# Attention scores with 64 rows of depth: two units at a time in TensorE's row halves

## What is computed

```
# first block: 8 heads of 64, three dilation patterns, written in the kernel as one masked softmax
scores = jnp.einsum('bhrnqd,bhrnkd->bhrnqk', qb, kc)
# even layer: 4 heads, each with two components of 64, and one context of 768 keys
def diff_attend(q, k, v, lam, scale):
    s = jnp.einsum('bqhcd,bkhcd->bhcqk', q, k).astype(jnp.float32) * scale
    p = jax.nn.softmax(s, axis=-1)
    w = (p[:, :, 0] - lam * p[:, :, 1]).astype(v.dtype)
    return jnp.einsum('bhqk,bkhd->bqhd', w, v)
```

## Time and profile before

| | us |
|---|---|
| median of 3 runs | 2516.4 |
| lowest and highest of them | 2516.34, 2520.65 |
| span of the profiled execution | 2514.0 |
| AT1, about | 219 to 315 |
| ATA, about | 596 to 706 |

### The profile page before, as it was taken

How to read it: one execution, slowest core, us unless ns; L and a number is a source line. 1 busy time by engine, 2 the same in 40 slices (tenths; PEclk the granted TensorE clock), 3 DMA queues, 4 the chain that set the end, 5 groups by cost and what they waited for, 6 DMA issues and landing times.

```text
span 2514.0 us, 26493 instructions
## 1 busy us (share of the span) xinstructions
PE 2214.4 (88%) x10170; PEld 1251.6 (50%) x10170; DVE 1298.6 (52%) x2310; ACT 978.0 (39%) x1609; POOL 459.6 (18%) x512
## 2 busy tenths in 40 slices
PE   6998998999888986999999997779999788777777
PEld 2444544446566444766676664446665333222222
DVE  2147526437875147889888985366662411111111
ACT  2024323114554035887888783355552100000000
POOL 0000000000133111454545420032221000000000
PEclk9999999999999997999999999889999889999999
DMA  7122611101000358999999997400032699999998
GB/s 279 67 74 93 226 44 38 67 17 68 1 1 1 135 222 301 358 370 367 373 378 367 380 357 282 171 8 1 1 134 103 248 382 404 407 404 404 402 412 345
DMA packets 92570, 546.29 MB, mean 217 GB/s; under 512 B 7807, under 2 KB 10639, under 8 KB 67614
## 3 DMA queue, kind: packets, MB, share of 16 engines
q1 hardware_dynamic: 84894, 521.02, 53.1%
q0 software_dynamic: 6144, 20.98, 3.7%
q10 hardware_dynamic: 1408, 2.62, 0.3%
HBM read 523.62 MB, written 20.97 MB: 217 GB/s over the span
## 4 chain that ended last, share of the span: by engine, by line
PE 23%; DMA 15%; DVE 11%; ACT 6%; issue 4%; POOL 1%; another core or an unknown queue 0%; SPq 0%; ACTq 0%; POOLq 0%; DVEq 0%
DMA AR<-in_w_exp_up_dram 8%; DVE RW L2087 7%; PE PS L2342 5%; PE PS L2121 5%; DMA AR<-in_w_exp_down_dram 4%; PE PS L684 3%; ACT AR L2175 3%; ACT RW L2079 2%; PE PS L985 2%; DMA AR<-in_w_exp_gate_dram 2%; PE PS L898 2%; PE PS L695 2%; PE PS L2536 1%; DVE AR L2294 1%; PE PS L2688 1%
## 5 line engine op out<-in xcount | busy, mean ns | idle before, releaser
L2087 DVE TENSOR_TENSOR RW<-AR,RW 128x2048 fp32r<-128x2048 f32 x192 | 432.5, 2285 | 45.6 <-ACT RW L2079 45.6
L2342 PE MATMUL PS<-AR 128*64 128x512 f32 x1536 | 363.1, 619 | 94.6 <-DMA AR<-in_w_exp_gate_dram 45.7
L2079 ACT CAST RW<-AR 128x2048 fp32r<-128x2048 f32 x192 | 364.1, 1912 | 121.0 <-PE PS L2121 107.4
L2121 PE MATMUL PS<-RW,RX 128*96 128x512 f32 x1536 | 363.1, 395 | 4.5 <-DVE RX L2227 4.0
L2121 PEld LDWEIGHTS PS<-RW,RX 128*96 128x96 f32 x1536 | 247.9, 162 | 110.7 <-issue 5.2
L2342 PEld LDWEIGHTS PS<-AR 128*64 128x64 f32 x1536 | 112.3, 141 | 321.2 <-issue 253.3
L2121 PE MATMUL PS<-RW,RA 128*96 128x512 f32 x768 | 186.6, 399 | 11.9 <-DVE RA L2284 11.9
L1713 PE MATMUL PS<-AR 128*128 128x512 f32 (+1 forms) x480 | 190.0, 552 | 0.7 <-ACT AR L620 0.7
L684 PE MATMUL PS<-AR 96*128 96x512 f32 (+3 forms) x480 | 183.5, 499 | 3.8 <-POOL AR L661 2.3
L784 DVE TENSOR_REDUCE AR<-PS 128x1 f32<-128x768 f32 (+1 forms) x160 | 135.9, 850 | 97.0 <-PE PS L684 78.7
L2419 POOL DMA_INDIRECT x_rows<-AR x16 | 119.0, 7439 | 351.7 <-DVE AR L2294 264.3
(11 more groups left out here) (346 smaller groups left out, 2684.3 us busy)
## 6 DMA issues: line engine op xcount, KB each, us to landing
AR<-in_w_exp_gate_dram SPq DMA_DIRECT2D x64, 2048.0 KB, 13.9
AR<-in_w_exp_up_dram SPq DMA_DIRECT2D x64, 2048.0 KB, 13.2
AR<-in_w_exp_down_dram SPq DMA_DIRECT2D x63, 2048.0 KB, 13.0
AR<-in_w_ada_dram SPq DMA_DIRECT2D x30, 2048.0 KB, 11.8
AR<-in_w_in_dram SPq DMA_DIRECT2D x6, 2048.0 KB, 9.1
AR<-in_w_in_even_dram SPq DMA_DIRECT2D x4, 2048.0 KB, 7.8
AR<-in_w_out_dram SPq DMA_DIRECT2D x2, 2048.0 KB, 7.9
AR<-in_w_out_even_dram SPq DMA_DIRECT2D x2, 2048.0 KB, 7.9
```

What stands on the lines that cost most here:

```text
L2079: s.copy(pair(i)[0], raw_half(key, hf)).then_inc(*S.up("hi", l, i))
L2087: v.tensor_tensor(lo, raw_half(key, hf), hi.bitcast(F32), ALU.subtract).then_inc(*V.up("split", key, hf))
L2121: m = pe.matmul(bank(ob)[0:Mc, :], st_, mv[:, k, 512 * q_:512 * q_ + 512], start=(k0 + k == 0 and n_ == 0), stop=(k0 + k == 7 and n_ == 2))
L2342: m = pe.matmul(bank(b)[64 * q_:64 * q_ + 64, :], op, w[:, c, 512 * q_:512 * q_ + 512], start=(h == 0 and c == 0), stop=(h == 1 and c == 3 ...
```

## The change

`pool_attn` and the cells are gone, and the two components (or two heads) of one query block are issued together by a new function. In an even step it waits for the banks of both units, and then issues for each slice of 512 keys one matmul of the upper unit with 64 rows at `tile_position` (0, 0) and one of the lower unit at (64, 0), into banks 0 or 1 and 2 or 3. Nothing is done for the scores in an odd step. In AT1 the order of units changes so that the two heads of a pair alternate within each query block: 128, 128, 256, 256, 384, 384, 512, 512 keys in place of 128, 256, 384, 512. The work of DVE and ACT on a unit, and their own order of steps, stay.

```diff
-        def pool_attn(A):
-            for i, u in enumerate(A.units):
-                r_ = u["row"]
-                if u["cell_before"]:
-                    G.wait_ge("full", "sc", *u["cell_before"])
-                u["ready"](G)
-                G.wait_ge("qz", 0)
-                g.tensor_copy(u["cell"][64 * r_:64 * r_ + 64, :], u["q"]).then_inc(*G.up("qp", A.tag, i))
+        def pe_scores_two(A, i):
+            for n_ in (i, i + 1):
+                u, p0 = A.units[n_], 2 * (n_ % 2)
+                K.fill(p0, "sc", A.tag, n_)
+                if u["nk"] > 512:
+                    K.fill(p0 + 1, "sc2", A.tag, n_)
+                    K.n[p0 + 1] -= 1
+                u["ready"](P)
+            nk = A.units[i]["nk"]
+            for a in range(0, nk, 512):
+                e_ = min(nk, a + 512)
+                m = [pe.matmul(PS[:, 2 * r_ + a // 512, 0:e_ - a], A.units[i + r_]["q"], A.units[i + r_]["k"][:, a:e_],
+                               start=True, stop=True, tile_position=(64 * r_, 0)) for r_ in range(2)]
+            for r_ in range(2):
+                m[r_].then_inc(*K.full("sc", A.tag, i + r_))
...
         def pe_attn(A, fill=None):
             n = len(A.units)
             for step in range(n + 4):
-                if step < n:
-                    pe_scores(A, step)
+                if step < n and step % 2 == 0:
+                    pe_scores_two(A, step)
...
-        for h in range(8):
-            for j in range(4):
-                r0, c = 64 * (h % 2), h // 2
-                units.append(dict(q=qT[r0:r0 + 64, c, 128 * j:128 * j + 128], k=kT[:, c, :], row=h % 2, vo=r0,
+        for h, j in [(2 * hp + r_, j) for hp in range(4) for j in range(4) for r_ in range(2)]:
+            r0, c = 64 * (h % 2), h // 2
+            units.append(dict(q=qT[r0:r0 + 64, c, 128 * j:128 * j + 128], k=kT[r0:r0 + 64, c, :], vo=r0,
...
-                    units.append(dict(q=QK[64 * c:64 * c + 64, h, 128 * j:128 * j + 128], k=QK[:, 4 + h, k0:k0 + nk],
-                                      row=c, nk=nk, dv=128, ready=QK_ready, vready=VV_ready,
+                    units.append(dict(q=QK[64 * c:64 * c + 64, h, 128 * j:128 * j + 128], k=QK[64 * c:64 * c + 64, 4 + h, k0:k0 + nk],
+                                      nk=nk, dv=128, ready=QK_ready, vready=VV_ready,
...
             g.memset(RB0, 0.0).then_inc(*G.up("rb0", 0))
-            pool_attn(AT1)
-            pool_attn(ATA)
             pool_pairs(ATB, lambda it: None)
```

More of the change, by code:

```diff
@@ L670, in pe_scores @@
             u["ready"](P)
-            if u.get("row") is not None:
+            if u.get("khl"):
                 P.wait_ge("qp", A.tag, i)
-            q = u["cell"] if u.get("row") is not None else u["q"]
-            if u.get("khl"):
                 at = 0
@@ L683, in pe_scores @@
                     e_ = min(nk, a + 512)
-                    m = pe.matmul(PS[:, p0 + a // 512, 0:e_ - a], q, u["k"][:, a:e_], start=True, stop=True)
+                    m = pe.matmul(PS[:, p0 + a // 512, 0:e_ - a], u["q"], u["k"][:, a:e_], start=True, stop=True)
             m.then_inc(*K.full("sc", A.tag, i))
@@ L1459, in program @@
         units = []
-        for h in range(8):
-            for j in range(4):
-                r0, c = 64 * (h % 2), h // 2
-                units.append(dict(q=qT[r0:r0 + 64, c, 128 * j:128 * j + 128], k=kT[:, c, :], row=h % 2, vo=r0,
-                                  nk=128 * (j + 1), moff=384 - 128 * j, dv=64, ready=qk_ready, vready=vv_ready,
-                                  v=lambda k, h=h: vv[:, k, 128 * (h // 2):128 * (h // 2) + 128],
-                                  out=OO[:, j, 64 * h:64 * h + 64]))
+        for h, j in [(2 * hp + r_, j) for hp in range(4) for j in range(4) for r_ in range(2)]:
+            r0, c = 64 * (h % 2), h // 2
+            units.append(dict(q=qT[r0:r0 + 64, c, 128 * j:128 * j + 128], k=kT[r0:r0 + 64, c, :], vo=r0,
+                              nk=128 * (j + 1), moff=384 - 128 * j, dv=64, ready=qk_ready, vready=vv_ready,
+                              v=lambda k, h=h: vv[:, k, 128 * (h // 2):128 * (h // 2) + 128],
+                              out=OO[:, j, 64 * h:64 * h + 64]))
         def fine(l, j):
```

## The result

| | before | after |
|---|---|---|
| median, us | 2516.37 | 2548.58 |
| lowest and highest | 2514.02, 2520.65 | 2546.02, 2551.27 |
| span of the profiled execution | 2514.0 | 2549.3 |

The ratio is 1.0124 (95% interval 1.0108 to 1.0139): 32 us slower. I had forecast 2530 (2518 to 2543), so the direction was right, the size less than half of what came, and the time lies outside the range.

A forecast was written before the change was run, and what follows sets the result against it. PE was taken to bound AT1, PE and DVE nearly both ATA. 2514.0 (span) + 2.4 (to the median) - 4 (AT1) + 11.3 - 0.8 + 2.8 + 0.5 + 4 (ATA) = 2530.2 us; range 2518 to 2543.

The forecast's parts named there:

- What bounds the kernel: PE sets the pace in AT1; in ATA PE and DVE are both close to full, with DVE next.
- the loop in ATA: Pair's scores wait for the second exponential, DVE for the scores: wide head 5.74 us against 4.93, +11.3 us in all.
- Splits: Four ATA heads with a key split: DVE waits longer for ACT, 4 x 0.7 = +2.8 us.
- those terms: ATA without the clock: wide heads +11.3, first pair's earlier start -0.8, key splits +2.8, narrow heads +0.5 us.
- Side by side: A pair's two row halves run at once: 1.3 us for a wide pair, against 2.6 without overlap.
- Rival 1: Row halves take turns: ATA's wide part +13, narrow +3, AT1 about +3, fewer clock falls; 2551 us, chance 0.12.
- The clock: PE's gaps in ATA cause four more falls to 1.2 GHz at 1 us: +4 us, between 0 and 9.
- AT1: First attention: scores save 3.6 net, a load costs 0.7, the start gains 1.0: -4 us, between -8 and 0.
- the order of units: In AT1, a load issued when fill work frees its slot makes PE wait about 0.7 us more.
- the waits behind ACT: In AT1, second transposes wait for ACT's copy: some 0.15 us in three of four pairs, 0.4 in 8 units.
- Rival 2: ATA's new wait costs little, the clock stays up, AT1 gives its whole 8 us: about 2519 us, chance 0.14.
- Rival 3: In ATA the pair's scores lie under DVE's own work, head 4.6 us: -5, AT1 -4; 2507 us, chance 0.06.

The follow-up runs named there:

- e3: e2 plus unread 128-column matmuls in PE's gaps of ATA (3 and 5 per wide head, 2 and 4 per narrow one): 2531.5 us.
- e2: The kernel before with paired row-half scores in ATA alone, AT1 keeping its cells and order: 2545.8 us.
- e1: The kernel before with paired row-half scores and the new order of units in AT1 alone, ATA unchanged: 2520.7 us.
- e6: The kernel before with only AT1's order of units changed, keeping cells, full array and single units (POOL gets a wait): 2519.7 us.
- e7: The kernel before with ATA paired in row halves and its loops rewritten by heads for pairs, AT1 as before: 2506.0 us.
- e4: The kernel before with each unit's scores alone on one row half in both attentions, no cells, old order and old waits: 2557.8 us.
- e14: ATA's single units in row halves in the old loop, two unread full-array matmuls added behind each transpose and product, AT1 as before: 2531.6 us, one run.

## Why the prediction was wrong in size

- **What bounds the kernel, and the loop in ATA: right.** The head came to 5.74 us and measured 5.77, PE's wait for the exponential (1.39) and DVE's for the scores (1.32) are where they were put. Splits were 0.5 to 0.6 us longer than the loop explains (7.3 to 7.6 in e3 against 5.9 to 6.2), against 0.7; three of the four lie in wide heads, one in the narrow part. With most of the clock's part gone, e3 is 14.7 us above before by the medians; those terms sum to 11.3 - 0.8 + 2.8 + 0.5 = 13.8.
- **Side by side: right.** Rival 1, halves taking turns, gave nearly the right time (2551), by luck and for the wrong reason; eight records in 1.56 us refute it, and a time alone would not have.
- **The clock: the mechanism right, the count wrong.** "I take four falls more at 1 us: +4 us". A fall in a wide head did cost 1.1 to 1.4 us (6.84 to 7.14 against 5.74). But eight of 15 intervals had one, and the narrow part stayed down for its last 22 us, "often" in the text and without a term of its own in the sum. e2 less e3 is 14.3 us by the medians (11.3 by ATA in the two profiled executions), above the bound of 9. The step that failed is going from the earlier trace rows, one stretch with PE busy 1.34 of 3.50 us, to a guess of four; the runs show a fall in every second wide head, 8 in all, and five narrow heads at 1.0 us more each (3.86 against 2.88, and 5.31 against 4.34 with the split). With 13 in place of 4 the sum would have been 2539.
- **AT1: wrong sign.** -4 us was predicted, +3.9 measured (e1). The working costed the order of units at 0.7 us for one load and the waits behind ACT at 0.15 us in three of four pairs. The order alone costs 4.2 (e6), and in e1 PE meets ACT's copy or DVE's masking, mostly at 0.6 to 1.7 us a time: 14.1 us in 11 waits, where before had 7.5 in 3. I followed one unit of 512 keys ahead of single pieces of fill work and took it for all 32; the loss in e1 is in the first 16 units, where ACT also has the recurrence and where fill work comes in other portions. The waits are shown; how much of the order's own cost they are is not, since about half of it lies behind unit 24, with a longer stretch at 1.2 GHz.
- The two terms make nearly the whole error: 10.3 us of clock and 7.9 of AT1 are 18.2, and the result lies 18.4 above the sum.
- **Rival 2** (waits cheap, AT1 gives 8) had nothing for it in the runs. **Rival 3** was rightly put at little for this loop, and its condition, scores under DVE's own work, was what e7 then built.

## What to carry to other kernels

Two small matmuls side by side also need their outputs' banks at the same time: what was a double buffer is none any more, and the engines behind must be given other work for the time of the exchange, or the gain turns into a wait on both sides. The same pairs in ATA cost 29 us in the old loop and gave 9.5 in one written for them. When PE's work shrinks in a loop that it does not bound, price the clock for every turn of the loop, not by a few falls, and try a few unread matmuls in the gap: if the kernel gets faster and the granted clock rises, the cause is shown. And a change of order "for free" is best run by itself before its cost is taken as nothing.

## What the runs showed of the hardware

- Float32 matmuls on two row halves run fully side by side: eight records in 1.56 us against 2.82 over the full array. The Trainium skill ("TensorE: Matmul & The Clock Gate", Part 3) says so of row tiles, and the trace agrees; in e4 a change to a row half and back costs 0.33 us.
- TensorE was busy 56.8 of 60 us and stayed at 1.2 GHz, with more than half of its work on 64 rows (e4); with 0.9 us more of full-array work in each head it came up after 20 us (e14, one execution). In the profiled execution of every kernel here it fell to 1.2 GHz in or behind 32 matmuls of 2 columns in which it was busy all the time (3.50 of 3.50 us before).
- Gaps of 1.4 us in every 5.8 brought the clock down in 8 of 15 heads. The Trainium skill's "A second HAM failure mode: psum-queue depth-cycling" on the same page describes short waits of the engine between groups of matmuls as enough for it; the trace agrees. The section "HAM oscillation", which the prediction names, tells of longer gaps, in which the engine waits for loads.
